# Two attentions in a new order of tiles: the first 512 tokens of all pairs, then the second, with norm, split and output products in between

## What is computed

```
q, gate, q_mem, g_mem = split(rms_norm(x) @ b_w_in)          # 768, 768, 256, 256 columns
for each of 6 heads (two sub-heads of 64, values of 128):
    p1, p2 = softmax(q1 k1 + bias), softmax(q2 k2 + bias)    # bias -slope*|distance|; keys of own and earlier 64-token chunks
    o = (p1 - lam * p2) @ v
y_br  = rms_norm_over_the_head(o) * subln * (1 - lam_init)   # norm over the 128 values of a head
y_mem = memory_cross_attention(q_mem, mem)                   # 2 pairs of heads
y = concat(y_br * silu(gate), y_mem * silu(g_mem)) @ w_out
x = x + rms_norm(y, post_norm)
```

## Time and profile before

| | us |
|---|---|
| runs | 3363.44, 3365.93, 3352.05; median 3363.44 |
| profiled execution, its own time | 3360.08 |
| its span | 3358.8 |
| mean granted TensorE clock | 0.934 of 2.4 GHz |
| second attention, from the last product before it | 2895.5 to 3176.5 |
| from there to the end | 182.3 |

### The profile page before, as it was taken

One profiled execution on the slowest core, in us unless ns is written; L12 is line 12 of the kernel. 1 busy time (PEld: TensorE's weight loads), 2 busy tenths in 40 slices (PEclk: granted clock), 3 DMA queues, 4 the chain that ended last, 5 costly groups with the idle time before them and its releaser, 6 DMA issues. The chain is left out here.

```text
span 3358.8 us, 49940 instructions
## 1 busy us (share of the span) xinstructions
PE 2869.6 (85%) x20746; PEld 2299.7 (68%) x20746; DVE 1713.3 (51%) x3034; ACT 988.9 (29%) x1803; POOL 688.4 (20%) x531
## 2 busy tenths in 40 slices
PE   7978878799999999689999867777758899998767
PEld 6766666588888888467788546666637678766545
DVE  3425555544444444675554167676644433467534
ACT  3214444311111111633221211121134222244543
POOL 2112233211101110252111022222112211122123
PEclk9988999899999999899999979899979899999978
DMA  3111032011111111122112100000022201010222
GB/s 105 45 50 39 14 101 69 25 57 44 51 50 44 44 57 45 38 79 84 38 39 66 46 1 3 3 3 3 23 93 82 94 20 51 27 38 29 83 77 76
DMA packets 196449, 162.45 MB, mean 48 GB/s; under 512 B 5200, under 2 KB 173818, under 8 KB 195458
## 3 DMA queue, kind: packets, MB, share of 16 engines
q1 hardware_dynamic: 196226, 159.26, 15.1%
HBM read 137.19 MB, written 22.05 MB: 47 GB/s over the span
## 5 line engine op out<-in xcount | busy, mean ns | idle before, releaser
L721 PE MATMUL ps<-r,r 128*128 128x512 f32 (+1 forms) x2304 | 944.0, 410 | 142.4 <-DVE r L686 115.4
L722 PE MATMUL ps<-r,r 128*128 128x512 f32 (+1 forms) x2304 | 914.5, 397 | 0.0
L723 PE MATMUL ps<-r,r 128*128 128x512 f32 (+1 forms) x2304 | 912.8, 396 | 0.0
L721 PEld LDWEIGHTS ps<-r,r 128*128 128x128 f32 x2304 | 446.4, 194 | 274.2 <-DVE r L686 128.9
L667 POOL TENSOR_TENSOR sb<-sb 128x1024 f32<-128x1024 f32 x138 | 280.6, 2039 | 1350.3 <-DMA sb<-in_w_ffn_up 488.6
L723 PEld LDWEIGHTS ps<-r,r 128*128 128x128 f32 x2304 | 445.4, 193 | 95.3
L722 PEld LDWEIGHTS ps<-r,r 128*128 128x128 f32 x2304 | 446.3, 194 | 92.3 <-issue 6.2
L2234 PE MATMUL ps<-sb 64*64 64x64 f32 (+2 forms) x8832 | 298.2, 225 | 122.3 <-DVE sb L2485 29.5
L2234 PEld LDWEIGHTS ps<-sb 64*64 64x64 f32 (+1 forms) x8832 | 277.3, 135 | 151.3 <-issue 99.3
L686 DVE TENSOR_TENSOR r<-sb,r 128x1024 fp32r<-128x1024 f32 x198 | 274.2, 1392 | 192.1 <-ACT r L681 191.7
L681 ACT CAST r<-sb 128x1024 fp32r<-128x1024 f32 x198 | 204.9, 1044 | 228.3 <-POOL sb L667 228.2
(11 more groups left out here) (276 smaller groups left out, 3604.8 us busy)
## 6 DMA issues: line engine op xcount, KB each, us to landing
sb<-in_w_out SPq DMA_DIRECT2D x36, 512.0 KB, 4.1
sb<-in_a_w_in SPq DMA_DIRECT2D x29, 512.0 KB, 4.0
sb<-in_w_ffn_gate SPq DMA_DIRECT2D x22, 512.0 KB, 3.9
sb<-in_w_ffn_up SPq DMA_DIRECT2D x22, 512.0 KB, 3.9
sb<-in_w_ffn_down SPq DMA_DIRECT2D x22, 512.0 KB, 3.4
sb<-in_w_in SPq DMA_DIRECT2D x17, 512.0 KB, 4.0
sb<-in_x SPq DMA_DIRECT2D x16, 512.0 KB, 5.5
xs<-sb SPq DMA_DIRECT2D x4, 2048.0 KB, 9.5
```

Of the source, the lines that this page charges most:

```text
L721: pe.matmul(self.out, w.hi[:, q, self.cols], hi, start=(q == 0), stop=False)
L722: pe.matmul(self.out, w.hi[:, q, self.cols], lo, start=False, stop=False)
L723: ins = pe.matmul(self.out, w.lo[:, q, self.cols], hi, start=False, stop=(q == w.nk - 1))
```

## The change

The tiles of both attentions run in another order: the tiles iq 0 to 3 of all pairs, then iq 4 to 7 of all pairs. The bias rows and the strip are set anew twice per pair. In layer b all 128 gate units stand in the first 24 tiles (`spread`: 6, 6, 5, 4 units per tile, 6, 6, 6, 5 in the last pair). In the following 24 tiles, between the steps of the attention, stand the norm of each head for the first 512 tokens (square at place 0 of tile 24 + j, sum, Ln and Exp at place 1 one tile later, scaling at place 0 two tiles later, gate product and split at place 3 three tiles later), the same for the second 512 tokens of heads 0 to 3, and from tile 33 on the 64 units of the eight output products of the first 512 tokens (4 or 5 a tile, bank 7, ring of 2). The split's low part is always POOL's. There is no `Join` after the attention. The gates come back in two transfers of 2 MB, asked for at tile 24. After the attention stand the norm and split of heads 4 and 5 for the second 512 tokens, the eight products of these tokens and the end as before. Tanh now resets `act_set`.

```diff
@@ EvictGate.act
+        self.k.act_set = None
         act.activation(self.gated, self.buf(st), ACT.Tanh).then_inc(*s.stage_tanh.up(st.id))
@@ Attention.__init__
+        self.seq = [(i, 4 * h + j) for h in range(2) for i in range(n) for j in range(4)]
...
+    def begins(self, i, iq):
+        return iq % 4 == 0
@@ ForgetBiasRows.sp_pair
+        if was := att.last_of_pair_before(i, iq):
+            sp.wait_ge(*s.bias_made.at((*was, 1)))
+        sp.dma_start(self.cb, ...).then_inc(*s.dma_cb.up(("cb", i, iq), 16))
@@ in place of SubNorm: SubSquare, SubRstd, SubScale, each for one head and 512 tokens
+class SubRstd(Step):
     def pe(self, pe):
+        pe.wait_ge(*s.sub_sq.at(of.id))
+        k.bank_free(pe, self.bank)
+        pe.matmul(k.ps[:, self.bank, :], k.ones, of.buf, start=True, stop=True).then_inc(*s.sub_sum.up(of.id))
+        k.free[self.bank] = ("step_act", ("sub_ln", of.id))
+    def act(self, act):
+        act.wait_ge(*s.sub_sum.at(of.id))
+        k.functions(act, LN_EXP_SET)
+        act.activation(of.buf, k.ps[:, self.bank, :], ACT.Ln, bias=k.eps, scale=1.0 / P)...
+        act.activation(of.buf, of.buf, ACT.Exp, scale=-0.5).then_inc(*s.sub_rstd.up(of.id))
@@ layer_b
+    ends = spread(k, put, prods, 0, [6, 6, 5, 4] * 5 + [6, 6, 6, 5], True)
+    for st, t in ends:
+        put(t + 1, 0, Gated(k, st))
...
+    put(turns, 3, *fetch)
+    sums = [[SubRstd(k, st, 6) for st in squares[h]] for h in range(2)]
...
+    for j in range(BT):
+        t = turns + j
+        put(t, 0, squares[0][j])
+        put(t + 1, 1, sums[0][j])
+        put(t + 2, 0, scales[0][j])
+        put(t + 3, 3, his[0][j], los[0][j])
+        t = turns + 4 * j + 5
+        if t + 3 <= last:
+            put(t, 0, squares[1][j])
...
+    for j in range(BT, KT):
+        put(turns + 1 + j - BT, 3, his[0][j], los[0][j])
+        put(turns + 9 + j - BT, 3, his[1][j], los[1][j])
...
+    begin = turns + BT + 3
+    n_turns = last + 1 - begin
+    spread(k, put, first, begin, [8 * KT * (j + 1) // n_turns - 8 * KT * j // n_turns for j in range(n_turns)], False)
...
+    for st in prods + first:
+        st.take_bank(7)
+    yield from [Ring(k, 2), *att.steps(fill), After(k, sp=[("turned_out", (att.id, BT - 1, ST - 1))]), Ring(k, 4)]
+    for group in (squares, sums, scales):
+        yield from [group[1][j] for j in late]
+    yield from [st for j in late for st in (his[1][j], los[1][j])]
+    second = [Product(k, ws[i] if i >= 6 else columns(k, A["w_out_2"][1], i * P), ops[1], ev_2, i, 1) for i in reversed(range(KT))]
@@ spread, in place of between
+    for n, count in enumerate(counts):
+        due += count
+        for place, share in ((0, 3), (1, 2), (2, 1)) if count > 3 else ((1, 2), (2, 1)):
+            units = []
+            while left and len(units) < -(-due // share) and (not units or units[0][0] is left[0][0]):
+                units.append(left.pop(0))
+            due -= len(units)
```

More of the change, by code:

```diff
@@ L1674, in steps @@
             out += fill(t, 1)
[L1675 removed]
+            for n in range(len(self.groups(*self.seq[t])) + 1):
                 out += part(Values, t, n)
@@ L1684, in groups @@
     def groups(self, i, iq):
-        g = i * self.per_pair + sum(self.heads * ((self.nkeys(j) // P + 3) // 4) for j in range(iq))
+        g = self.first_group[i, iq]
         nj, out = self.nkeys(iq) // P, []
@@ L3096, in finish_layer @@
     yield from weave(first, (1, back[:1]), *by(3, splits[1], 1), (6, back[1:]))
[L3097 to L3106, removed]
+    yield from chain(k, ev, y, acc, second, back=[st.event() for st in back])
 def layer_b(k):
@@ L3157, in layer_b @@
                     ready=lambda i, iq: of_v + [("copied_dve", st[i, h]) for h in range(2) for st in (of_q, of_key)])
[L3158 to L3166, removed]
-    by_tile = ([4, 4, 4, 4, 3, 3, 2, 0], [4, 4, 3, 3, 2, 0, 0, 0])
-    places = {0: [], 1: [2], 2: [1, 2], 3: [0, 1, 2], 4: [0, 1, 2, 2]}
-    table, left = {}, 0
-    for t in range(BT * ST):
-        for place in places[by_tile[t // ST >= 4][t % ST]]:
-            if units:
-                table.setdefault((t, place), []).append(units.pop(0))
-    assert not units
-    def fill(t, place):
-        out = [Gated(k, st) for st in later.pop((t, place), ())]
-        for st, group in itertools.groupby(table.get((t, place), ()), key=lambda unit: unit[0]):
-            part = Part(k, st, [q for _, q in group], act_later=True)
-            out.append(part)
-            if part.last:
-                later.setdefault((min(t + 1, BT * ST - 1), 3 if t + 1 == BT * ST else 0), []).append(st)
-        return out
-    later = {}
-    return fill
@@ new lines, in layer_b @@
+    table = {}
+    fill = lambda t, place: table.get((t, place), [])
+    put = lambda t, place, *steps: table.setdefault((t, place), []).extend(steps)
+    turns = len(att.seq) // 2
+    ends = spread(k, put, prods, 0, [6, 6, 5, 4] * 5 + [6, 6, 6, 5], True)
+    for st, t in ends:
+        put(t + 1, 0, Gated(k, st))
+    stored = [(f"dma_stage{j}", prods[j - 2].id) for j in range(2)] + [("linear", prods[-1].id)]
+    mix = k.at(X, KT, S)
+    gates = [k.at(k.XL + HALF, KT, S)[:, :, 0:HALF], k.at(k.XH, KT, S)[:, :, HALF:S]]
@@ new lines, in layer_b, with spread @@
+    adds = [residual(k, h, y=y[h], r=acc[h], rstd_id=norms[h].id) for h in range(2)]
+    rows = k.at(F + 8192, 4, D)
+    store = [Store(k, i, rows, [("x_added", (adds[i // 4][0].key, KT - 1))] if i % 4 == 0 else []) for i in range(ST)]
+    there = [After(k, pool=[st.event()]) for st in back]
+    yield from weave(second, (1, [norms[0], there[0]]), *by(2, adds[0], 1), (6, back[1:]), (6, store[:2]), (7, store[2:4]))
+    yield from [norms[1], there[1], *adds[1], *store[4:]]
+def spread(k, put, prods, begin, counts, act_later):
+    left, due, ends = [(st, q) for st in prods for q in range(st.units())], 0, []
+    for n, count in enumerate(counts):
[5 more added lines that the diff above has]
+            due -= len(units)
+            if units:
+                st = units[0][0]
+                put(begin + n, place, Part(k, st, [q for _, q in units], act_later))
+                if units[-1][1] == st.units() - 1:
+                    ends.append((st, begin + n))
+    assert not left, len(left)
+    return ends
```

170 lines of the change are left out of this document (106 added, 64 removed).

## The result

The changed kernel takes 3381.14 us (median of 6 runs, 3377.88 to 3385.78), the kernel before 3361.40 (6 runs beside them, 3352.05 to 3365.93). The ratio of the means is 1.0064, 95% interval 1.0047 to 1.008: 0.64% slower. The forecast was 3354, with "same" (within 0.5%) as the likeliest class. The measured time lies outside the forecast's own range (3340 to 3368) and inside the wide one (3318 to 3388) that most of rivals A and B add; "slower" had been given 0.22. One execution of twelve in a later experiment (reductions at the tile's end) took 5692.74 us in a slow state and is left out of its median.

What follows compares the result with a forecast made beforehand. TensorE was busy 85% of the span; 61 us of non-product time after the second attention could be won. Attention +90 and the part after it -96 took 3360.1 to 3354 us; own range 3340 to 3368, wide 3318 to 3388.

Steps and rivals of the forecast that it cites:

- rival A: Whole kernel faster, waits covered: roundings cost 8 instead of 29.5, clock 2 instead of 8; 3319 us, chance 0.32.
- Rival B: Second attention, tiles 24 to 47: idle of about 2.9 us drops TensorE to 1.2 GHz; +30, 3384 us, chance 0.18.
- TensorE's own work in tiles 0 to 23: Second attention, first 24 tiles: small tiles' own work plus gate units, six pairs and two units more, 134 us.
- the clock beside the rounding waits: Second attention, tiles 33 to 47: lower clock after long waits, 1.4 us seven times with some missed, 8 us.
- First attention, 0: First attention (mixer): new order with eight bias-row loads instead of four costs 0 us, bounds -3 and +6.
- Tiles 0 to 23, 147: Second attention, first 24 tiles with all 128 gate units: 134 us of work and units plus 13 of waits, 147.
- Tiles 24 to 32, 72: Second attention, nine large tiles without units: chain latency 51 us plus reductions, table load, gates' wait and slow clock, 72.
- The wait for the gates: Second attention, near tile 25: DVE waits for the gates' 2 MB transfer back, 4 us (0 to 9).
- Rounding waits, 29.5: Second attention, tiles 33 to 47: TensorE waits for weight rounding before seven output products, 29.5 us, bounds 8 and 34.
- After the attention, 86.5: From the second attention's end to the span's end: remaining norm, second-half products and last norm, 86.5 us against 182.3.
- The table mark: Last norm: resetting the mark at Tanh removes its two table loads, one coming early instead; 2.6 us gained.
- three signs of being wrong: Part after last output transpose outside 80 to 93 us, rounding waits under 15, or attention's granted clock under 0.88.

Runs made afterwards that it cites:

- reductions at the tile's end: Changed kernel with seven of the ten norm reductions moved to the end of the tile, on bank 7 instead of bank 6: 3368.01 us, ratio 1.0024 to before.
- whole tiles: Changed kernel with the gate units of the first 24 tiles dealt 8, 4, 4 a tile instead of 6, 6, 5, 4: 3369.62 us, ratio 1.0029 to before.
- early rounding: Changed kernel with weight roundings for the first 512 tokens' output products placed half a product earlier: 3344.94 us, ratio 0.9958 to before.

## Why the prediction was wrong

Its waits were right, its sum was not. The forecast said -6 where +20 was measured, and three terms carry nearly all of it: TensorE's own work in tiles 0 to 23, the clock beside the rounding waits, and the part after the attention.

- **First attention, 0:** right; its order alone, undone, changed nothing.
- **Tiles 0 to 23, 147:** the step that failed most, by 13. The waits were sized well (13; idle measured 13.2, and 11.4 of it go with whole tiles). Mis-sized was the sum of TensorE's own work and units, 134, or 132.5 from the first scores; busy time there is 145.4. It counted six times a pair of four tiles and left out the start: the output transpose of tile 0 comes 12.0 us after the first scores, where a tile later takes 5.65 (22.6 per four with whole tiles). That is 6.4. The kernel before has such a start too, 9.9 us with fewer units in it (2896.99 to 2906.88), so its profile had shown it. Another 3.5 us are busy time that goes with the waits (145.4 against 142.0 in whole tiles). The lower clock was charged in the other two parts of the attention and not here. The remaining 3 us are not assigned.
- **Tiles 24 to 32, 72:** right in the sum (72.6) and near in the reductions (2.0 each; 11.9 us came back from moving seven, 1.7 each). The wait for the gates came (5.69, forecast 4), but its removal shortened nothing in the sum of the nine tiles.
- **Rounding waits, 29.5:** 29.8 in seven places, and rival A (8) was ruled out by them. The sum agrees better than its terms, which is luck: six waits are 3.51 to 4.17 (forecast 3.8 to 4.4) and one is 7.46 (forecast 5). The clock beside them was put at 8 and is 13.9: the early rounding gives back as much in busy time of the same matmuls. With the waits, 158.3 instead of 152.
- **After the attention, 86.5:** measured 92.6. The first two products end 20.7 after the last transpose (forecast 17.5), the rounding wait is 4.83 (4), the other six products with the norm and the stores between take 39.3 (37.3), the last norm 27.8 (26.5). The terms as written add up to about 85, not 86.5, so the sum itself hid 1.4. With the rounding early for these products too the part takes 84.2; the terms without the 4 for that wait are 81, so the rest is about 3 short. How the 8.5 between 92.7 and 84.2 divide was not tested singly. The rows, in TensorE's timeline:

```profile
3296.78 0.47 PE L724 MATMUL ps<-r,r 128*128 128x512 f32 x1 [2.15 <-POOL r L1417]
...
3313.05 0.79 PE L724 MATMUL ps<-r,r 128*128 128x512 f32 x1 [4.83 <-DVE r L688]
...
3353.76 1.12 PE L581 MATMUL ps<-sb 128*128 128x512 f32 x2 [1.41 <-DVE sb L929]
```

- **The table mark:** the loads at the last norm are gone, as forecast. Not seen: without the reset they would have come at every norm.

Rival B named the lower clock, and its figure of 3384 is close to the 3381 measured, but not for its reason: it put the price on nine unfilled tiles as well, and there the granted clock is 0.93. Its condition, waits past 2.9 us, fits the rounding waits only (the longest wait in tiles 24 to 32 is 2.6). None of the three signs of being wrong appeared: the part after the attention took 92.6 (80 to 93 allowed), the rounding waits sum to 29.8 (over 15), and the clock over the attention is 0.93 in the mean (over 0.88), though in tiles 33 to 47 alone it is 0.87. No sign watched the length of the attention, 391 from the last product before it where 371 was forecast.

The chances were wrong in a way that the sum could have told: a gain of 96 and a cost of 90, each with an error of several per cent, leave a difference whose sign is open. 0.22 for slower was too little; every part came out at or above its forecast, so the misses added up instead of cancelling.

## What to carry to other kernels

When work is moved under another stage, look at what the producer engines do directly before each first use. Here a weight rounded right behind its predecessor's eviction turned a gain of 0.4% into a loss of 0.6%. Place each such step half a product earlier, end each accumulation where another engine has free time before its bank is wanted, and keep foreign work out of the chain between two dependent copies. Count the start of a pipeline beside its steady steps, and where waits are charged, charge the lower clock behind them in every stage, not in some.

## What the runs showed of the hardware

- Seven waits of 3.5 to 7.5 us went with a granted clock of 0.87 over a stretch of 158 us; without them it was 1.00, and 13.9 us of busy time went with 23.0 of idle.
- The same ten value matmuls after 0.66 and after 0.55 us of wait took 1.35 and 2.47 us in two kernels that differ in that stretch only in where two gate products with their splits stand: the clock depends on more than the last wait.
- The stage of the first attention ended between 436 and 453 us in eight profiles of kernels with identical code there. Between 262 and 436 us the granted clock was 0.99 where it ended at 436.25, 0.91 at 444.97, 0.88 at 448.20 and 0.84 at 453.12. There is one profile of each kernel, so how often this happens is not known.
